# Experts of two latent tiles by a streamed table and dense gates, the other tiles by gathers

## The chip, the cores and the metric

One core of a Trainium2 chip. The metric is the device time of the whole program in microseconds. The program is one launch; all operands are fp32.

## The reference

One step of a layer for two groups of tokens: one tile of 128 context tokens and four tiles of 128 latent tokens, D_MODEL 1024. Two mixers (a gated recurrence and a windowed attention) and an output projection come first; the part that the change touches is the last one, a mixture over 16384 single-row experts, of which each token uses 16 in each of 8 heads:

```python
def per_block(xb):                      # 128 tokens
    q = (xb @ w_q).reshape(n, P_HEADS, 2, P_QDIM // 2)
    s = jnp.einsum('nhpd,hpkd->nhpk', q, sub_keys)
    s1, i1 = lax.top_k(s[:, :, 0], P_TOPK)
    s2, i2 = lax.top_k(s[:, :, 1], P_TOPK)
    cand_s = s1[..., :, None] + s2[..., None, :]
    cand_i = i1[..., :, None] * P_NKEYS + i2[..., None, :]
    top_s, pos = lax.top_k(cand_s, P_TOPK)         # both reshaped to (n, 8, 256)
    idx = jnp.take_along_axis(cand_i, pos, axis=-1)
    g = jax.nn.softmax(top_s, axis=-1)
    act = gelu(einsum('nhkd,nd->nhk', w_u[idx], xb))
    return einsum('nhk,nhkd->nd', g * act, w_v[idx])
```

Then x = x + gate2 * that, and a final RMSNorm. An expert's number is i1 * 128 + i2. w_u and w_v have 16384 rows of 4 KB, 64 MiB each.

## The kernel before

Five instruction streams (PE, ACT, DVE, POOL and SP) are written by hand and meet in semaphores. The order of PE's work is one list of names (`NAMES`, from `plan_groups`): each name is one accumulation group in PSUM, such as `("y", q, t)` (a 256-column quarter of the output projection of tile t), `x2T` and `h2` (transposes around the second norm), `qp` and `ss` (queries and scores of one half of a head). Groups take PSUM banks 0 to 3 in turn, and whoever evicts a group frees its bank.

Weights come as slabs of 1 MiB through a ring of three slots in SBUF (`SLABS`, issued by SP; a slot is loaded again when PE has finished the last group that reads it).

The experts are done by slots. A slot is one (head, k) of one tile: 128 indices, one for each token. POOL issues an indirect DMA that brings the rows `[u | v]` of the 128 experts, 128 x 8 KB; DVE makes the dot product of u with h2 (`dot`, line 1412, into `apre`); ACT makes the gelu (line 957) and the weight (line 963, `wexp`); then v times the weight is added up. For tile 0 and every other slot of the first half of tile 1, DVE does this (`v_row`, line 1440); elsewhere ACT makes a diagonal matrix of the weights (line 973) and PE multiplies it with the v rows into PSUM (line 600, and 587 in the first half of tile 1). One tile has 128 slots, the five tiles 640.

A head's indices and gates come from `route_parts`, 12 parts on DVE (max, max_index, match_replace over the scores, sums of candidates, and two 128 x 864 products with a compare to pick the expert's number); they are laid between the slots of the heads before.

Slots that run beside other work are placed by `STAGES`: a stage is a stretch of the list of names with a count of slots and a share for each kind of name, and every engine does slot n before the name where the plan puts it (`Beside`). ACT and DVE have slots and groups in one program order. Tile 0's 128 slots run beside the latent tiles' input projection, mixers and mix. 64 slots of tile 1 run beside `post(1)` (tile 1) and `post(2)` (tiles 2, 3, 4). Then come loops with the last 448 slots alone, with eight gather buffers, three of them in the slab ring. Gathers beside other work have four buffers (`NGA`) for tile 0 and six for tile 1. `tile_end(t)` adds the result to x and does the final norm, five operations of 128 x 1024.

Of the kernel before, what the change touches and what calls it, by code (L numbers as in the profile page):

```python
# [54 lines left out]
NGA, NGC, NGB = 4, 6, 8  # L55
HSTATIC = 4
NPE = HSTATIC * TOPK // 2
HSLOTS = 2 * TOPK
# [11 lines left out]
BATCHES = [(0,), (1,), (2, 3, 4)]  # L70
MIXES = [(0,), (1, 2, 3, 4)]
NSLOT = TSLOT + HSTATIC * TOPK
# [6 lines left out]
FIRST_ODD = 9  # L79
# [9 lines left out]
POOL_LEAD, PE_LAG = 3, 2  # L89
# [3 lines left out]
for _b in range(len(BATCHES)):  # L93
    if _b < len(MIXES):
        for _q in range(4):
            SLABS += [("gate_a", _b, _q), ("gate_b", _b, _q), ("wo", _b, _q)]
    SLABS += [("wout", _b, _q) for _q in range(4)] + [("wpq", _b, _q) for _q in range(8)]
    if _b == 0:
        SLABS += [("winTL", w, m) for w in WIN_T for m in range(2)] + [("winL", w, a) for w, a in WIN]

# [19 lines left out]
def turn_order(tiles):  # L120

    order = []
    for i in range(len(tiles) + 1):
        order.extend([("x2T", tiles[i])] if i < len(tiles) else [])
        order.extend([("h2", tiles[i - 1])] if i else [])
    return order


def plan_groups():
# [35 lines left out]
    def post(b):  # L165
        tiles = BATCHES[b]
        names.extend(("y", q, t) for q in range(4) for t in tiles)
        names.extend(turn_order(tiles))
# [34 lines left out]
    for b in (1, 2):  # L203
        marks.append(len(names))
        post(b)
    marks.append(len(names))
    marks.insert(-2, names.index(("ss", 1, FIRST_ODD)))
    place, used, fulls, n, six = {}, [0] * 6, [0] * 6, 0, 0
    for name in names:
        kind = name[0]  # L210
        wide = kind in ("xT", "kT", "dS", "qkT", "x2T", "h2") or (kind in ("sc", "pT") and name[1] >= HB)
# [27 lines left out]
    for (_, count, share), lo, hi in zip(STAGES, marks, marks[1:]):  # L239
        reach = np.cumsum([share[names[i][0]] for i in range(lo, hi)])  # L240
# [14 lines left out]
def build(nc, x_prompt, x_sample, cols, rows, normf_rows, brow, consts, masks, sel, cond_rows, ada_slabs, col_slabs, in_slabs, o_slabs,  # L255
          out_slabs, pq_slabs, uv, state, ckT, cv, y_prompt, y_sample, new_state, new_k, new_v):
    with ExitStack() as ctx:
# [17 lines left out]
        R1 = sb("R1", [P, 4 * D])  # L275
# [5 lines left out]
        RG = sb("RG", [P, 3 * 2 * D])  # L281
        BP = sb("BP", [P, NT * 256 + 6 * 512])
        AB = sb("AB", [P, 12288])
        HG = sb("HG", [P, 5632])
# [4 lines left out]
        CT = sb("CT", [P, P + 640 + NCAND])  # L289
# [6 lines left out]
        hst = sb("hst", [P, 16])  # L296
        ast = sb("ast", [P, 168])
        ZB = sb("ZB", [P, P], BF16)
# [6 lines left out]
        ident, mbias, iota = CT[:, 0:P], CT[:, P:P + 640], CT[:, P + 640:P + 640 + NCAND]  # L305
# [60 lines left out]
        XN2 = [view(HG, 0, D), view(HG, D, D)]  # L366
        SQ2 = [view(HG, 4096, D), view(HG, D, D), view(HG, D, D)]
        QP = [view(HG, 5120, 2, P), view(HG, 4096, 2, P), view(HG, 4096, 2, NB[2])]
        X1 = [XP] + [AB[:, 6144 + i * D:6144 + (i + 1) * D] for i in range(4)]
        H2 = [PB[:, 0:D]] + [AB[:, at:at + D] for at in (0, 3072, 4096, 5120)]  # L370
        SC = [R1[:, 0:2048], HG[:, 2048:4096], R1[:, 0:2048], AB[:, 10240:12288], AB[:, 1024:3072]]

# [151 lines left out]
        def _(sp):  # L524
# [1392 lines left out]
```

## Time and profile before

| | us |
|---|---|
| median of 3 runs | 2536.47 |
| lowest, highest | 2534.52, 2538.31 |
| span of the profiled execution | 2543.3 |

No time of its own is recorded for the profiled execution beside its span, from the first to the last instruction; the span lies 6.8 us above the median. Busy time in it: PE 2005.6 us (79%), DVE 1749.4 (69%), ACT 945.2 (37%), POOL 941.2 (37%). DMA moved 805.53 MB. In the slices of the page each digit is a fortieth of the span, 63.6 us. A matmul of fp32 appears as two records.

### The profile page before, as it was taken

To read this page: it belongs to the slowest core of one execution; us is meant where nothing else is said; L and a number is where in the kernel's file an instruction comes from. 1 tells how busy PE (TensorE), PEld (TensorE's weight loads), DVE (VectorE), ACT (ScalarE), POOL (GpSimd) and SP (SyncE) were. 2 spreads that over 40 slices of the span, in tenths; PEclk is the share of its full clock that TensorE was granted. 3 is DMA by queue.
4 is the path that set the end of the run, shared out by engine and by line. 5 is a ranking of instruction groups with operands and counts; after the bars stand their busy time and mean duration, and the time that the engine had idled before them with its cause. 6 is when DMAs were issued, how large, how long until landed. Compare 5 with 4: busy or idle time off the path is not lost. (4 is left out here: it accounts for less than half of the span.)

```text
span 2543.3 us, 27323 instructions
## 1 busy us (share of the span) xinstructions
PE 2005.6 (79%) x6925; PEld 1104.9 (43%) x6925; DVE 1749.4 (69%) x3969; ACT 945.2 (37%) x2456; POOL 941.2 (37%) x774
## 2 busy tenths in 40 slices
PE   6978898946677798668698776877768787687876
PEld 2577846745566543267455222322223222232222
DVE  2732278886776678767787777777777777777764
ACT  1402145223343434312333444444444444344443
POOL 0020012232222222303233554656545665456654
PEclk9998999977888899879899998999999999999999
DMA  8744678851111389859798999999999999999997
GB/s 317 289 152 154 231 291 322 332 192 67 67 67 60 150 332 337 337 203 401 272 372 317 422 421 393 420 422 422 421 404 415 422 422 421 407 401 421 422 422 330
DMA packets 113299, 805.53 MB, mean 317 GB/s; under 512 B 12596, under 2 KB 14006, under 8 KB 17046
## 3 DMA queue, kind: packets, MB, share of 16 engines
q0 software_dynamic: 93760, 680.96, 66.5%
q1 hardware_dynamic: 17704, 118.17, 12.6%
q10 hardware_dynamic: 1712, 4.98, 0.5%
q8 instruction: 50, 0.82, 0.1%
q14 instruction: 73, 0.60, 0.1%
HBM read 800.79 MB, written 3.28 MB: 316 GB/s over the span
## 5 line engine op out<-in xcount | busy, mean ns | idle before, releaser
L1213 POOL DMA_INDIRECT RG<-in_uv,idxs x264 | 356.5, 1351 | 562.0 <-DVE pl L1440 322.1
L957 ACT ACTIVATE agel<-apre 128x1 f32<-128x1 f32 x640 | 129.3, 202 | 984.6 <-DVE apre L1412 981.2
L600 PE MATMUL pl<-RG,BP 128*128 128x512 f32 x576 | 294.9, 638 | 106.8 <-ACT BP L973 102.3
L600 PE MATMUL pl<-RING,BP 128*128 128x512 f32 x576 | 281.7, 621 | 62.1 <-ACT BP L973 59.6
L1412 DVE CUSTOM_DVE_ANT_0 R<-RG,AB 128x1024 f32<-128x1024 f32 x201 | 246.8, 1230 | 100.8 <-DMA RG<-in_uv,idxs 79.8
L1213 POOL DMA_INDIRECT RING<-in_uv,idxs x168 | 248.9, 1482 | 158.7 <-PE pl L600 69.4
L1412 DVE CUSTOM_DVE_ANT_0 R<-RING,AB 128x1024 f32<-128x1024 f32 x168 | 205.9, 1226 | 95.6 <-DMA RING<-in_uv,idxs 77.2
L625 PE MATMUL pa<-HL,RING 128*128 128x512 f32 (+2 forms) x800 | 243.7, 461 | 4.2 <-DVEq L457 2.6
L600 PEld LDWEIGHTS pl<-RG,BP 128*128 128x128 f32 x576 | 100.1, 192 | 294.5 <-ACT BP L973 214.0
L973 ACT ACTIVATE BP<-CT,wexp 128x128 f32<-128x128 f32 x480 | 192.7, 401 | 51.1 <-PE pl L600 12.9
L600 PEld LDWEIGHTS pl<-RING,BP 128*128 128x128 f32 x576 | 104.3, 194 | 234.2 <-ACT BP L973 139.7
L963 ACT ACTIVATE wexp<-agel,gws 128x1 f32<-128x1 f32 x640 | 188.7, 295 | 22.4 <-ACT agel L957 0.3
L625 PEld LDWEIGHTS pa<-HL,RING 128*128 128x128 f32 x800 | 134.5, 195 | 106.0 <-issue 74.3
L1213 POOL DMA_INDIRECT EB<-in_uv,idxs x88 | 118.3, 1345 | 147.0 <-DVE pl L1440 96.8
L1440 DVE SCALAR_TENSOR_TENSOR pl<-RG,wexp,pl 128x1024 f32<-128x1024 f32 x118 | 151.6, 1285 | 9.6 <-ACT wexp L963 9.5
L1412 DVE CUSTOM_DVE_ANT_0 R<-RG,BP 128x1024 f32<-128x1024 f32 x96 | 117.7, 1226 | 43.4 <-DMA RG<-in_uv,idxs 27.6
L1412 DVE CUSTOM_DVE_ANT_0 R<-EB,AB 128x1024 f32<-128x1024 f32 x67 | 82.4, 1229 | 60.1 <-DMA EB<-in_uv,idxs 58.0
L625 PE MATMUL pa<-RING,AB 128*128 128x256 f32 (+2 forms) x432 | 103.9, 390 | 14.8 <-DVEq L457 10.3
L600 PE MATMUL pl<-HL,BP 128*128 128x512 f32 x192 | 94.9, 617 | 24.9 <-ACT BP L973 22.2
L957 ACT ACT_TABLE_LOAD x86 | 110.3, 1283 | 9.9 <-ACT RING L1096 2.8
L600 PE MATMUL pl<-EB,BP 128*128 128x512 f32 x192 | 98.8, 639 | 11.1 <-ACT BP L973 11.1
L625 PEld LDWEIGHTS pa<-RING,AB 128*128 128x128 f32 (+1 forms) x432 | 82.9, 201 | 34.1 <-issue 17.3
(288 smaller groups left out, 3261.0 us busy)
## 6 DMA issues: line engine op xcount, KB each, us to landing
RING<-in_in_slabs SPq DMA_DIRECT2D x42, 1024.0 KB, 6.0
RING<-in_pq_slabs SPq DMA_DIRECT2D x24, 1152.0 KB, 5.5
RING<-in_ada_slabs SPq DMA_DIRECT2D x16, 1024.0 KB, 5.0
RING<-in_out_slabs SPq DMA_DIRECT2D x12, 1024.0 KB, 9.1
RG<-in_col_slabs POOLq DMA_DIRECT2D x8, 1024.0 KB, 6.9
RING<-in_o_slabs SPq DMA_DIRECT2D x8, 1024.0 KB
RG<-in_uv,idxs POOLq DMA_INDIRECT x297
RING<-in_uv,idxs POOLq DMA_INDIRECT x168
```

The lines of the kernel that those rows point to most:

```text
L600: last = nc.tensor.matmul(acc[:, c * 512:(c + 1) * 512], DG[:, k % 2, :], bufs[k % len(bufs)][:, D + c * 512:D + (c + 1) * 512], start=Fal ...
L625: return nc.tensor.matmul(out, l, r, start=s, stop=e)
L957: A(agel[:, par, k:k + 1], apre[:, par, k:k + 1], ACT.Gelu).then_inc(gel_done, 1)
L963: A(wexp[:, par, k:k + 1], agel[:, par, k:k + 1], ACT.Copy, scale=gws[:, par, k:k + 1]).then_inc(w_done, 1)
L973: A(DG[:, i % 2, :], ident, ACT.Copy, scale=wexp[:, par, k:k + 1]).then_inc(dg_done, 1)
L1213: nc.gpsimd.indirect_dma_start(out=bufs[b], out_offset=None, in_=uv, in_offset=bass.IndirectOffsetOnAxis(ap=idxs[:, par, k:k + 1], axis=0) ...
L1412: V.tensor_tensor_reduce(out=SCR[k % 2], in0=buf[:, 0:D], in1=hc, scale=1.0, scalar=0.0, op0=ALU.mult, op1=ALU.add, accum_out=apre[:, par, ...
L1440: V.scalar_tensor_tensor(PL[:, :], (GC[i % NGC] if t else GA[n % NGA])[:, D:2 * D], wexp[:, n // TOPK % 2, n % TOPK:n % TOPK + 1], PL[:, : ...
```

## The change

- Tiles 2 and 4 (`DENSE`) don't gather any more. All 16384 experts are computed for their 256 tokens, in 128 chunks; chunk c holds the 128 experts whose second key is c, one for each partition (first key). `u_slabs` and `v_slabs` are the two tables laid out by chunk, two chunks a slab, and go through the slab ring after the other weights.
- `experts_u(c)`: 8 matmuls of 256 columns and a gelu on ACT into `AR`, a ring of 50 chunks in SBUF. `experts_v(c)`: 4 matmuls of 512 columns that add `AR` times v into PSUM banks 4 to 7.
- The gates: routing in DVE (`dense_route`, with the expert's number kept as a value); `slots_of` splits the number in two keys; PE turns the three tables so that tokens lie on columns (`T`); for each token, POOL makes a one-hot of the first keys times the weight (`OH1`, for the odd groups of tile 4 DVE does it, `drawn`), DVE one of the second keys (`OH2`), and one matmul of 128 columns (`G`, four tokens a group) gives the 128 x 128 gates of the token. ACT puts them in a staging buffer, 16 tokens with all chunks, and stores it to DRAM (`gates`), 1 MiB at a time, with 16 tokens inside and the chunks outside. SP loads them block by block (16 chunks of one tile, 1 MiB), and DVE multiplies them into `AR` (`weigh`, 2048 elements a partition).
- Tiles 1 and 3 gather all their 128 slots, each with dot and v row on DVE, in four buffers; PE and the diagonals have no part in slots any more. 256 slots follow those of tile 0: 26 beside `post(2)`, 24 beside the stage `early`, 206 beside the stage `dense`.
- `BATCHES` are (0), (1, 2), (3, 4). The scores are copied by ACT. x of the latent tiles is stored to DRAM and loaded again near the end. `tile_end(0)` stands before `post(1)`; tile 1's in the middle of the slots; tiles 3, 2 and 4 at the end.

The core of the diff:

```diff
+NGA, NGD = 4, 4
+DENSE, GATHERED = (2, 4), (0, 1, 3)
+NCH, NEARLY, NRING = NKEYS, 34, 50
+NFREE = 24
+GBLK, GTOK = 16, 16
-BATCHES = [(0,), (1,), (2, 3, 4)]
+BATCHES = [(0,), (1, 2), (3, 4)]
...
-          ("post1", 0, {"y": 3.5, "x2T": 2.0, "h2": 2.0, "qp": 2.0, "ss": 1.0}),
-          ("queries1", 4, {"qp": 2.0, "ss": 0.1}),
-          ("post2", 60, {"y": 3.4, "x2T": 2.5, "h2": 2.5, "qp": 5.2, "ss": 1.2}))
+          ("post1", 0, {}),
+          ("post2", 26, {"y": 3.4, "x2T": 2.5, "h2": 2.5, "qp": 5.2, "ss": 1.2}),
+          ("early", 24, {"U": 3.4, "T": 1.0, "G": 1.6}),
+          ("dense", 206, {"V": 1.0, "U": 1.0}))
+NAHEAD = 3
+SLABS += [("dU", p) for p in range(NRING // 2)]
+for _p in range(NCH // 2):
+    SLABS += [("dV", _p)] + ([("dU", _p + NRING // 2)] if _p + NRING // 2 < NCH // 2 else [])
...
+    at = {("dU", NEARLY // 2 + 2): [(0, 0), (0, 1)], ("dU", NRING // 2 - 2): [(1, 0)], ("dU", NRING // 2 - 1): [(1, 1)]}
+    for b in range(2, NBLK):
+        for i, back in enumerate((7, 6)):
+            at[("dV", GBLK // 2 * b - back)] = [(b, i)]
...
+DENSE_AT = {("U", 2 * (d - NAHEAD)) if d < PH else ("G", 0, 4 * (d - PH)): d for d in range(NAHEAD, 2 * PH)}
...
+def early_order():
+    order, c = [("U", n) for n in range(10)], 10
+    for i in range(ND):
+        order.append(("T", i))
+        for h in range(PH):
+            order.extend(("G", i, 4 * h + x) for x in range(4))
+            upto = 10 + 14 * (h + 1) // PH if i == 0 else NFREE + (NEARLY - NFREE) * (h + 1) // PH
+            order.extend(("U", n) for n in range(c, upto))
+            c = upto
+    return order + [("U", n) for n in range(NEARLY, NRING)]
...
+            def gate_slab(b, i):                                   # SP
+                n = b * ND + i
+                if n == 0:
+                    wait_full(sp, ("G", ND - 1, P // 4 - 1))
+                    for s in stage_out:
+                        sp.wait_ge(s, 16 * (ND * P // GTOK // 2))
+                if n >= 2:
+                    sp.wait_ge(p_done, n - 1)
+                sp.dma_start(GS[n % 2], gates[b, i]).then_inc(gate_in[n % 2], 16)
...
+            def experts_v(c):                                      # PE
+                w = slab("dV", c // 2)[:, c % 2 * D:(c % 2 + 1) * D]
+                if c % GBLK == 0:
+                    pe.wait_ge(p_done, ND * (c // GBLK + 1))
+                for i in range(ND):
+                    for x in range(2):
+                        last = nc.tensor.matmul(VACC[i][:, x * 512:(x + 1) * 512], AR[:, c % NRING, i * P:(i + 1) * P],
+                                                w[:, x * 512:(x + 1) * 512], start=c == 0, stop=c == NCH - 1,
+                                                skip_group_check=True)
+                last.then_inc(vd_done, 1)
...
+            def gates_out(i, g):                                   # ACT
+                to = STG[s].rearrange("p b (c t) -> p (b c) t", c=GBLK)[:, :, g % 4 * 4:g % 4 * 4 + 4]
+                step(A(to, ps.rearrange("p (t n) -> p n t", t=4), ACT.Copy), *freed(("G", i, g)))
+                if g % 4 == 3:
+                    at = g // 4 * GTOK * GBLK
+                    act.dma_start(gates[:, i, :, at:at + GTOK * GBLK].rearrange("b p n -> p b n"),
+                                  STG[s]).then_inc(stage_out[s], 16)
...
+                for x in range(ONEHOT):                            # POOL, slot_hots
+                    at = q * ONEHOT + x
+                    step.post(nc.gpsimd.tensor_scalar(OH1[n % 2][:, x, :], iota_p, SLT[i][:, 0, at:at + 1],
+                                                      SLT[i][:, 2, at:at + 1], ALU.is_equal, ALU.mult))
...
+            def weigh(b, i):                                       # DVE
+                dve.wait_ge(act_ready, GBLK * (b + 1))
+                dve.wait_ge(gate_in[n % 2], 16 * (n // 2 + 1))
+                gate = GS[n % 2].rearrange("p (a c t) -> p c a t", c=GBLK, t=GTOK)
...
+                    step(V.tensor_tensor(to, to, gate[:, lo:lo + m], ALU.mult))
...
+            for name in early_order():                             # DVE
+                if name[0] == "T" or name in DENSE_AT:
+                    beside.before(name)
+                    beside.clear()
+                if name in DENSE_AT:
+                    dense_route(DENSE_AT[name])
+                if name[0] == "T":
+                    weights_of(PH * (name[1] + 1) - 1)
+                    slots_of(name[1])
+                if name[0] == "G" and name[2] % 2 == 0:
+                    beside.before(name)
+                    gate_hots(name[1], name[2] // 2)
+            beside.before(("U", NRING - 4))
+            weigh(0, 0)
+            weigh(0, 1)
...
+            for b in range(2, NBLK):
+                beside.before(("V", GBLK * b - 8))
+                weigh(b, 0)
+                weigh(b, 1)
+            beside.rest()
+            for e in range(2, NT):
+                tile_end(e)
```

## Rows read from the trace of the kernel before

**Rows 1.** The page: busy time, slices of DMA and GB/s, the last chain.

```profile
span 2543.3 us, 27323 instructions
...
DMA  8744678851111389859798999999999999999997
GB/s 317 289 152 154 231 291 322 332 192 67 67 67 60 150 332 337 337 203 401 272 372 317 422 421 393 420 422 422 421 404 415 422 422 421 407 401 421 422 422 330
...
DMA 15%; issue 9%; DVE 5%; POOL 5%; PE 3%; ACT 2%; DVEq 0%; POOLq 0%; ACTq 0%
```

**Rows 2.** Windows: length, busy by engine, PE clock, DMA share, GB/s.

```profile
1386.00:2530.00 1144.00, 892.10 (x1847) 324.82 (x1846) 818.90 (x1983) 495.55 (x1467) 654.28 (x448) 0.97 1.00 414
950.00:1050.00 100.00, 88.37 (x199) 37.42 (x198) 79.67 (x128) 38.05 (x77) 27.18 (x26) 0.97 0.91 341
1097.00:1386.00 289.00, 253.22 (x1073) 177.15 (x1072) 221.16 (x518) 84.72 (x235) 68.91 (x65) 0.93 0.83 320
```

**Rows 3.** Timeline of PE at post(1): start, length, records.

```profile
1094.58 16.55 PE L625 MATMUL pa<-RING,AB 128*128 128x256 f32 x64
1115.12 1.97 PE L628 MATMUL pa<-CT,HG 128*128 128x128 f32 x8 [3.99 <-DVEq L457]
...
1121.05 4.94 PE L625 MATMUL pa<-HL,RING 128*128 128x128 f32 x32
```

**Rows 4.** Timeline of PE, runs of 256, 512 and 128 columns.

```profile
499.50 7.07 PE L625 MATMUL po<-RING,HL 128*128 128x256 f32 x32
506.41 7.07 PE L625 MATMUL pa<-RING,HL 128*128 128x256 f32 x32
...
1295.11 1.88 PE L587 MATMUL po<-EB,BP 128*128 128x512 f32 x4
1296.83 0.83 PE L625 MATMUL pa<-RING,HG 128*128 128x128 f32 x6
```

**Rows 5.** Timeline of DVE, a slot with dot and v row.

```profile
363.08 1.23 DVE L1412 CUSTOM_DVE_ANT_0 R<-RG,BP 128x1024 f32<-128x1024 f32 x1 [0.25 <-DVE idxs L1379]
...
365.43 1.22 DVE L1412 CUSTOM_DVE_ANT_0 R<-RG,BP 128x1024 f32<-128x1024 f32 x1
```

**Rows 6.** Timeline of DVE, route(0), 34 operations; first, compare and last.

```profile
323.14 0.29 DVE L1350 COPY BP<-R 128x256 f32<-128x256 f32 x1
323.58 0.29 DVE L1332 MAX8 BP<-BP 128x8 f32<-128x128 f32 x1
...
332.30 1.06 DVE L1372 TENSOR_TENSOR BP<-CT,BP 128x864 f32<-128x864 f32 x1
...
336.09 0.23 DVE L1389 TENSOR_SCALAR gws<-BP 128x16 f32<-128x16 f32 x1
```

**Rows 7.** DMA issues of the page: the norm row, median us to landing.

```profile
R<-in_normf_rows ACTq DMA_DIRECT2D x5, 512.0 KB, 7.9
```

**Rows 8.** Groups of POOL: busy us, mean ns.

```profile
L1263 POOL TENSOR_SCALAR HG<-AB 128x512 f32<-128x512 f32 x4 | 2.5, 619 | 11.7 <-PE pa L628 11.7
...
L1255 POOL TENSOR_TENSOR CO<-HG 128x4 f32<-128x4 f32 x5 | 1.0, 200 | 0.4
```

**Rows 9.** Timeline of DVE and SP, the last `tile_end` and store.

```profile
2534.30 1.23 DVE L1698 TENSOR_TENSOR R<-pl,G 128x1024 f32<-128x1024 f32 x1 [3.59 <-PE pl L894]
...
2538.87 1.28 DVE L1706 SCALAR_TENSOR_TENSOR AB<-AB,st,R 128x1024 f32<-128x1024 f32 x1
2540.24 0.33 SPq L570 DMA_DIRECT2D out<-AB  x1
```

**Rows 10.** Windows with slabs and gathers mixed, columns as in rows 2.

```profile
1144.00:1208.00 64.00, 56.16 (x269) 45.33 (x268) 49.06 (x124) 15.41 (x46) 20.59 (x20) 0.95 0.99 401
1290.00:1340.00 50.00, 50.00 (x172) 29.39 (x171) 43.12 (x100) 16.08 (x47) 18.26 (x16) 1.00 0.98 382
```

**Rows 11.** Timeline, one gather buffer's turn: v row, issue, dot.

```profile
1057.21 1.28 DVE L1440 SCALAR_TENSOR_TENSOR pl<-EB,wexp,pl 128x1024 f32<-128x1024 f32 x1
1058.49 1.22 DVE L1412 CUSTOM_DVE_ANT_0 R<-RG,BP 128x1024 f32<-128x1024 f32 x1
...
1064.85 1.23 DVE L1412 CUSTOM_DVE_ANT_0 R<-EB,BP 128x1024 f32<-128x1024 f32 x1 [0.39 <-DMA EB<-in_uv,idxs]
...
1059.30 1.22 POOL L1213 DMA_INDIRECT EB<-in_uv,idxs  x1 [2.90 <-DVE pl L1440]
```

**Rows 12.** The dots' line from 930 to 1090 us, and SP's issues.

```profile
L1412 DVE DVE_READ_ACCUMULATOR2_ANT apre<- x42: 76/83/85, 932.9 to 1088.4; 128x1 f32 x42
...
1026.73 74.40 SPq L558 DMA_DIRECT2D RING<-in_out_slabs  x4
```

More of the change, by code:

```diff
@@ L475, in open, with clear @@
             def open(self, t):
-                self.first, self.end = t * TSLOT, min((t + 1) * TSLOT, NSLOT)
+                self.first, self.end = (0, TSLOT) if t == 0 else (TSLOT, NSLOT)
+            def clear(self):
+                while self.next < self.end and self.next % TOPK in (3, 4):
+                    self.slot(self.next)
+                    self.next += 1
             def rest(self):
@@ L513, in half_update, with drawn, pool_hots, block_of @@
             yield mul(tots[:, set_of(u), d, :] if l == LEVELS - 1 else HT[d][l % 2][:, 0:n], T2[:, :, 0], T2[:, :, 1])
+        def drawn(i, q):
+            return i == ND - 1 and q % 2 == 1
+        def pool_hots(i, q):
+            return sum(not drawn(a, b) for a in range(ND) for b in range(P // ONEHOT) if (a, b) < (i, q)) + 1
+        def block_of(i, g):
+            n = i * (P // GTOK) + g * 4 // GTOK
+            return n % 2, n // 2
         slab_turn, counts = {}, [0] * NSLAB
@@ L889, in post, with experts_u @@
                     finish(("ss", b, m), last)
[L891 to L897 removed]
+            def experts_u(c):
+                w = slab("dU", c // 2)[:, c % 2 * D:(c % 2 + 1) * D]
+                ps = start(("U", c))
+                for k in range(KD):
+                    last = mm(ps[:, 0:DTOK].rearrange("p (t n) -> p t n", t=ND), w[:, k * P:(k + 1) * P],
+                              hTl[:, k, :].rearrange("p (t a n) -> p t a n", t=ND, a=2)[:, :, 1, :], k == 0, k == KD - 1)
+                finish(("U", c), last)
@@ L1143, in post, with scores_out @@
                         step(A(H2[t], ps, ACT.Copy), *freed(("h2", t)), h2_ready)
+                def scores_out(m):
+                    ps = group(("ss", b, m))
+                    for i, t in enumerate(tiles):
+                        step.post(A(SC[t][:, m * NKEYS:(m + 1) * NKEYS], ps[:, i * NKEYS:(i + 1) * NKEYS], ACT.Copy))
+                    step.settle(*freed(("ss", b, m)), sc_ready)
                 if b == 1:
-                    tile_root(0)
+                    act.wait_ge(v_done, TSLOT + V0)
+                if b == 2:
+                    act.wait_ge(x1_early, 32)
                 for m in range(2 * PH):
@@ L1802, in _ @@
             beside.rest()
+            tile_end(0)
+            post(1)
+            dve.wait_ge(kv_out, 32)
+            dve.wait_ge(sc_ready, 2 * PH + 2)
+            route(PH, 0, 12)
+            dve.wait_ge(sc_ready, 2 * PH + 4)
+            route(PH + 1, 0, EARLY)
+            step(V.memset(ACC, 0.0))
+            for d in range(NAHEAD):
+                dense_route(d)
             beside.open(1)
-            post(1)
             post(2)
-            beside.rest()
-            dve.wait_ge(h2_ready, NT)
@@ L1838, in shape_constants @@
+            beside.before(("U", NRING - 4))
+            weigh(0, 0)
+            weigh(0, 1)
+            beside.before(("V", 4))
+            weigh(1, 0)
+            weigh(1, 1)
+            for b in range(2, NBLK):
+                beside.before(("V", GBLK * b - 8))
+                weigh(b, 0)
+                weigh(b, 1)
+            beside.rest()
+            for e in range(2, NT):
+                tile_end(e)
 def shape_constants():
```

720 lines of the change are left out of this document (371 added, 349 removed).

## The prediction

> **What bounds the kernel now.** I read the page first. Its slices [rows 1] show three regimes: up to the twentieth slice DMA is mostly unsaturated, then two slices of change, and from the 23rd on DMA is at 9 tenths with 401 to 422 GB/s, while PE, DVE, ACT and POOL all have gaps. The chain that ended last says the same: its largest share is DMA, in gathers. Next the windows by stage [rows 2]: from 1386 us to 2530 us the DMA share is 1.00 at 414 GB/s, DVE is busy 72% and PE 78%. So the tail, 45% of the span, is a pure gather stream: 448 of the 640 slots (a slot is one expert row of u and v for each of 128 tokens, 128 x 8 KB = 1 MiB) at 1 MiB / 422 GB/s = 2.49 us each. Before it, from 1097 to 1386 us, the work after the mixers (output projection, second norm, queries) runs at 320 GB/s beside the first 64 slots of tile 1. Nothing before 1094 us depends on the change except ACT instead of DVE copying the scores of tile 0 and a few moved buffers: I cost that at nothing (the copies wait for PE either way; the bound is a microsecond or two either side).
>
> **What the change trades.** From 1094.6 us, where PE starts `y` of tile 1 [rows 3], before moves 512 MiB of gathers and 26 MiB of weight slabs. After moves 256 MiB of gathers (tiles 1 and 3), 26 of weights, 64 of u and 64 of v as slabs, 16 of gates out, 16 of gates in and some 6 of small things: 448 MiB = 470 MB. At 422 GB/s that is 1113 us against 1337. But half of the v rows move from PE to DVE, and tiles 2 and 4 bring new work on PE, so I go stage by stage, since the plan ties slots to PE's groups (ACT does both in one order, so neither may run far ahead).
>
> Unit costs. U chunk: 8 matmuls of 256 columns; 32 records (16 matmuls, each recorded twice) take 6.91 us to the next start [rows 4], so a chunk takes 3.45 us. V chunk: 4 matmuls of 512 columns; two take 1.72 us [rows 4], so 3.45 us. A 128-column matmul: 0.22 us [rows 4]. A gathered slot on DVE is now always dot and v row: 363.08 to 365.43 us, 2.35 us [rows 5], plus some 0.15 of waits. A head's routing run without a break takes from 323.14 to 336.3 us [rows 6]; the change drops the first copy (0.44 us): 12.8 us for a gathered head; a dense one drops the index cast too and adds nothing else: 12.5 us. So a gathered slot costs 2.5 + 12.8/16 = 3.3 us of DVE.
>
> **Stage A, post(1) with tiles 1 and 2, no slots.** PE: 8 groups `y` 27.7 us; the turn through the norm 9.9 us for one tile (1111.1 to 1121.05 [rows 3]), 12 for two; 16 x (3.45 + 0.44) = 62 us queries and scores. 1094.6 + 102 = 1197 us. `tile_end(0)` now stands ahead of `y` on DVE and waits for the norm row (7.9 us to landing [rows 7], formerly hidden): DVE is free at about 1106 us; PE fills its four banks until 1108 us, so this costs nothing; at worst 5 us. DVE then does route(8), half of route(9), a memset and three dense routes, from 1143 us when the first two scores are there: 12.8 + 6.5 + 0.9 + 37.5 gives 1201 us. Even with PE.
>
> **Stage B, post(2) with tiles 3 and 4, 26 slots.** PE 102 us again, from 1201; `y` is slowed by five slots between its reads, and the 19 slots beside the queries cost DVE 19 x 3.3 = 63 us, as much as PE's 62. End about 1310 us.
>
> **Stage C, 50 U chunks and the gates, 24 slots.** PE: 50 x 3.45 + 256 gate matmuls x 0.22 = 229 us. DVE: 13 dense routes x 12.5 = 162; 19 slots before the last gate group x 3.3 = 63; 32 one-hots of 128 x 1024: a form like the 864 wide compare, 1.06 us [rows 6], scaled 1.25 + 0.1 = 1.35, 43 us; 8 x 2 more for the drawn ones, 22; the slots of two tiles made ready and turned, with the round trips through PE and ACT, 11 by estimate (ten 128 wide operations of some 0.3 us a tile [rows 6] and 2.5 us of trip). Sum 301 us. So C is DVE's: 1310 + 301 = 1611 us for the last gate group; PE waits at `T`. POOL builds 24 x 8 one-hots; an operation of 512 wide takes 0.62 us [rows 8], 128 wide between 0.2, the smallest POOL row [rows 8], and 0.62: at most 5 us per eight tokens against DVE's 9 per eight: hidden (if not, 24 x a few us). Then PE has 16 U chunks left, 55 us, and ahead of chunk 38 SP's queue holds the first two gate loads, which wait for the last gate store: some 10 us of bubble. V starts at about 1678 us.
>
> **Stage D, 128 V and 78 U chunks, 206 slots.** Three bounds. PE: 206 x 3.45 = 711 us. DVE: 206 x 3.3 = 680, `weigh` 16 x 2.4 (2048 elements, twice the 1.22 us of a 1024 wide one [rows 9]) = 38, `tile_end(1)` 8: 726. DMA: 206 gathers, 39 + 64 slabs, 12 gates, 2 for x: 323 MiB, less 6 already in flight or landed: 317 MiB = 332 MB. At the 422 GB/s of the tail's slices [rows 1] 788 us. So DMA bounds D whatever it does, and the question is the rate. Rows for mixed traffic [rows 10]: 401 GB/s at a share of 0.99 (1144 to 1208 us, gathers in six buffers with slabs), 382 at 0.98 (1290 to 1340), 341 at 0.91 in the mix stage [rows 2], where gathers have four buffers as they will here: 829, 870 and 975 us. D keeps three slab slots and four gathers wanting all the time, and both other engines are at 0.86 to 0.88 of its length, so I take the row where DMA was really full, 401: 829 us.
>
> Do four buffers let it be full? The buffer's v row is done one slot after its dot, so only three gathers run ahead. From the v row's end at 1058.49 to the gather's issue at 1059.30 is 0.8 us, from there to its dot at 1064.85 us 5.55 us [rows 11], with DMA lightly loaded; dot and v row 2.4 more: 8.8 us for three slots, 2.9 us a slot. D wants 829/206 = 4.0 us a slot, 12 us for three, so each gather may stand 3 us in the queue behind a slab. That is enough for a steady stream, not for the 5 us of two `weigh`.
> The Trainium skill ("DMA: Bandwidth & Descriptors", the section on issuing engines) says that transfers started by scalar, sync and gpsimd run on the same 16 engines and interleave. By that rule slabs and gathers share one rate, as I have them; a second stream on top would leave D at 726 us, and no run here shows such a thing.
>
> **The end.** After the last gather: dot, weight, v row 3 us; three `tile_end` in a row instead of one, 2534.30 to 2540.15 = 5.9 us each [rows 9], 18; store 3: 24 us.
>
> **Sum.** 1678 + 829 + 24 = 2531 us against the span of 2543.3. The profiled execution lies 6.8 us above the median of 2536.5 shown, so I take the same off: about 2525 us, 0.5% faster. Most of the 224 us that the smaller traffic would give are lost because A to C move only some 130 MiB in 583 us.
>
> **Rivals.**
> 1. D at a mixed rate of 390 to 422 GB/s, as forecast: D 788 to 851 us, 2484 to 2547 us. For it: the 64 us at 401. Chance 0.5 (0.4 of it faster, 0.1 within 0.2%).
> 2. Slower: the four gather buffers and the lock step through ACT leave DMA idle part of the time. For it: the mix stage, also with four buffers, where 42 dots took 160 us, 3.8 us each, at 341 GB/s [rows 12]. Against: slabs were rare there, four in 74 us [rows 12], so nothing else filled the gaps. At 341 to 385 GB/s D takes 862 to 975 us: 2558 to 2671 us. It decides from 393 GB/s downward (2542 us). Chance 0.3. The skill's page on DMA (Bandwidth) gives about 358 GB/s as what HBM leaves one core; by that D would take 927 us and end near 2623; the tail's 422 GB/s disagrees, and I give it no chance of its own.
> 3. Slower: C is longer. If POOL's one-hots cost more than 0.62 us each, or DVE waits for ACT's exponentials, gelus and slots in turn, 30 to 60 us more: 2555 to 2585. Against: hots are double buffered and routes stand between. Chance 0.1.
> 4. Clearly faster: A to C end 30 us or more earlier, because PE runs its U chunks under the routes, and D runs at 422: 2440 to 2470 us. Chance 0.1.
>
> **Numbers.** The likeliest is 2525, its own range 2484 to 2547. 0.2% (5 us) is about what a measurement of this kernel can tell from no change. Faster 0.4 + 0.1 = 0.5, same 0.1, slower 0.3 + 0.1 = 0.4. For 8 in 10 I go from 2470 to 2605 (365 GB/s in D).
>
> **What would show it.** `V` starting near 1678 us; in C, DVE nearly full and PE waiting for it; in D, DMA share at 0.95 or more with 390 to 405 GB/s, DVE and PE both near 0.85, and dots that wait for gathers. Wrong it is if D's share of DMA is well under 0.95 (rival 2: buffers, or who waits for whom), if PE waits in C for POOL, if slabs and gathers together pass 405 GB/s, or if `weigh` over its 16-element runs takes far more than 2.4 us, 16 times on the path of V.

## The result, and the profile after

The changed kernel takes 2715.1 us (median of 4 runs, 2711.5 to 2722.9) against 2535.5 us: a ratio of 1.0708, 95% interval 1.0689 to 1.0727. It is 7.1% slower, where I had forecast 2525 us and a range up to 2605. Two of the runs below, with five buffers and with the shifted slots, had one execution each in a slower state (4211.9 and 3080.0 us), which their times here leave out.

The page of the changed kernel: slices of 1/40 of the span, the chain that ended last by engine, and two of its groups (count | busy us, mean ns | idle before, and its releaser):

```profile
span 2710.9 us, 28055 instructions
...
DMA  7836598722113998444932445689999899999996
GB/s 310 294 115 220 204 351 331 277 92 70 63 47 141 352 344 311 140 187 171 384 142 93 155 148 187 234 333 385 397 359 393 338 401 359 391 377 381 383 351 234
...
DMA 28%; DVE 25%; PE 21%; issue 16%; POOL 7%; ACT 2%; DVEq 1%; POOLq 0%; ACTq 0%; SPq 0%
...
L1371 POOL DMA_INDIRECT R<-in_uv,idxs x288 | 323.1, 1122 | 1138.5 <-DVE AB L1620 729.5
...
L710 PE MATMUL pa<-XS,EB 128*128 128x128 f32 x512 | 92.0, 360 | 130.5 <-POOLq L530 73.8
```

The slices answer [rows 1]: the flat 420 GB/s of the gather stream from the 23rd slice on has gone. In its place stand ten slices (17th to 26th) in which DMA is at 2 to 6 tenths but for one, and then a stretch at 8 to 9 tenths that moves 338 to 401 GB/s, where the kernel before moved 393 to 422 (its 25th slice has 393, which I had read over). POOL stood idle 729.5 us for v rows before it could issue gathers into `R`, and the gate matmuls (`pa<-XS,EB`) waited 73.8 us for POOL's queue. The windows of the changed kernel (us, then busy time of PE, PEld, DVE, ACT, POOL, then granted clock, DMA share, GB/s), gate stage and V stage, to be held against [rows 2]:

```profile
1445.00:1729.00 284.00, 170.52 (x865) 155.06 (x866) 186.26 (x410) 78.27 (x149) 216.98 (x193) 0.79 0.47 157
1791.00:2659.00 868.00, 749.19 (x2275) 447.46 (x2274) 612.43 (x1044) 157.80 (x522) 214.16 (x199) 0.94 0.95 374
```

**Where the 180 us are.** My sum was 2531 us against this span of 2710.9. For the milestones I split it where the trace can be read. `T` of tile 2 was due at 1388 us (my 1310 for the end of `post(2)`, five dense routes, three slots and half of the 11 us for turning the slots) and comes at 1427 (+39). From there to the end of the last gate group remain 223 us of my sum; it takes 302, to 1729 (+79). The U chunks between it and the first V take 62 us instead of 67 (-5). From the first V to the end of the last slot I had 829 us; it is 1791 to 2690, 899 (+70). The end is 21 us instead of 24 (-3). These are +180. Milestones of single traces are not exact to a microsecond: in the three later runs that change only what the V stage loads, gathers or weighs, the first V starts between 1799.9 and 1803.5 us, here at 1791.5.

Each large term has its cause in a few rows. First, VectorE in route(8), the last operation of part 10 and the first of part 11:

```profile
1147.40 0.17 DVE L1510 CAST idxs<-BP 128x16 int32<-128x16 f32 x1
1188.51 0.16 DVE L1514 RECIPROCAL BP<-BP 128x1 f32<-128x1 f32 x1 [40.93 <-ACT BP L1063]
```

VectorE stands idle for 40.93 us until ScalarE has made the exponential of head 8. ScalarE's program now does the whole of `post(1)`, all sixteen evictions of queries and scores, before `expos(PH)`. Then TensorE at the seam of post(1) and post(2), and at `T`:

```profile
1185.96 13.98 PE L710 MATMUL pa<-RING,AB 128*128 128x256 f32 x64
1234.92 16.54 PE L710 MATMUL pa<-RING,AB 128*128 128x256 f32 x64 [34.98 <-DVEq L530]
...
1427.09 0.90 PE L713 MATMUL pa<-CT,BP 128*128 128x128 f32 x3 [21.55 <-DVEq L1550]
1445.36 4.82 PE L710 MATMUL pa<-XS,EB 128*128 128x128 f32 x29 [17.37 <-issue]
```

It has filled four banks with `y` of `post(2)` and waits 35 us for VectorE, which is still routing: that is the first term. Second, the operations of POOL's one-hots (count: min/median/max ns, first and last start):

```profile
L1384 POOL TENSOR_SCALAR EB<-CT,BP x128: 780/790/2545, 1431.5 to 1595.5; 128x128 f32<-128x128 f32 x128
L1384 POOL TENSOR_SCALAR EB<-CT,RW x64: 785/1402/2543, 1608.6 to 1722.6; 128x128 f32<-128x128 f32 x64
```

and VectorE's waits from 1326 to 1785 us (us in total, times, longest):

```profile
DVE AB L1620 <- ACT wexp L1081: 54.6, 7, 15.6
DVE XS L1567 <- PE pa L710: 42.3, 14, 6.9
```

A weighted one-hot of 128 x 128 costs 0.79 to 1.40 us in the median, not at most 0.62: eight take 7.9 us by the mean in tile 2's half and 11 in tile 4's (10.9 for those at 1623 us). TensorE waits for them, and VectorE for TensorE (42.3 us) to free the one-hots' buffers. Third, one turn of a gather buffer in the V stage, on VectorE:

```profile
1964.70 1.28 DVE L1620 SCALAR_TENSOR_TENSOR AB<-R,wexp,AB 128x1024 f32<-128x1024 f32 x1
...
1975.70 1.23 DVE L1594 CUSTOM_DVE_ANT_0 R<-R,BP 128x1024 f32<-128x1024 f32 x1 [0.83 <-DMA R<-in_uv,idxs]
...
1981.10 1.28 DVE L1620 SCALAR_TENSOR_TENSOR AB<-R,wexp,AB 128x1024 f32<-128x1024 f32 x1
```

and on POOL:

```profile
1966.79 0.94 POOL L1371 DMA_INDIRECT R<-in_uv,idxs  x1 [2.74 <-DVE AB L1620]
```

The v row ends at 1965.98, the gather into its buffer is issued 0.8 us later, the dot on it starts 8.9 us after the issue (5.55 in [rows 11]), and the v row that frees the buffer again ends at 1982.38: four slots in 16.4 us, 4.1 us each.

### The profile page after: what moved, and what is told of

Its sections match the earlier page's. It is cut to its first block, busy times and chain, and to the rows that moved or that the text cites. A ratio compares the mean times of both kernels' runs of the same rounds, so it can differ in the third digit from the quotient of the medians.

```text
span 2710.9 us, 28055 instructions
## 1 busy us (share of the span) xinstructions
PE 2071.8 (76%) x8515; PEld 1462.2 (54%) x8515; DVE 1788.0 (66%) x3622; ACT 702.1 (26%) x1719; POOL 714.6 (26%) x713
## 4 chain that ended last, share of the span: by engine, by line
DMA 28%; DVE 25%; PE 21%; issue 16%; POOL 7%; ACT 2%; DVEq 1%; POOLq 0%; ACTq 0%; SPq 0%
DMA R<-in_uv,idxs 23%; PE pa L710 18%; POOL EB L1384 6%; DVE AB L1620 5%; DMA AB<-in_uv,idxs 4%; DVE pl L1620 4%; PE po L710 1%; PE pa L713 1%; DVE AB L1585 1%; DVE AB L1749 1%; DVE AB L1757 1%; DMA RING<-in_ada_slabs 1%; DVE BP L1499 1%; DVE BP L1496 1%; DVE apre L1594 1%
## 5 line engine op out<-in xcount | busy, mean ns | idle before, releaser
L710 PE MATMUL pa<-HL,RING 128*128 128x256 f32 (+1 forms) x2848 | 735.3, 417 | 103.6 <-ACTq L530 100.5
L710 PEld LDWEIGHTS pa<-HL,RING 128*128 128x128 f32 x2848 | 559.9, 200 | 279.1 <-issue 206.5
L1371 POOL DMA_INDIRECT R<-in_uv,idxs x288 | 323.1, 1122 | 1138.5 <-DVE AB L1620 729.5
L1594 DVE CUSTOM_DVE_ANT_0 R<-R,BP 128x1024 f32<-128x1024 f32 x192 | 235.5, 1227 | 139.6 <-DMA R<-in_uv,idxs 98.8
L1620 DVE SCALAR_TENSOR_TENSOR AB<-R,wexp,AB 128x1024 f32<-128x1024 f32 x192 | 246.1, 1282 | 56.9 <-ACT wexp L1081 56.8
L994 PE MATMUL po<-RING,AB 128*128 128x512 f32 x512 | 244.5, 600 | 36.0 <-DVEq L1587 36.0
L994 PE MATMUL pl<-RING,AB 128*128 128x512 f32 x512 | 241.4, 594 | 0.0
L710 PE MATMUL pa<-XS,EB 128*128 128x128 f32 x512 | 92.0, 360 | 130.5 <-POOLq L530 73.8
L710 PE MATMUL pa<-RING,AB 128*128 128x256 f32 (+3 forms) x528 | 125.0, 386 | 81.2 <-DVEq L530 77.4
L1384 POOL TENSOR_SCALAR EB<-CT,BP 128x128 f32<-128x128 f32 x128 | 124.6, 983 | 18.2 <-PE pa L710 16.5
L1620 DVE SCALAR_TENSOR_TENSOR pl<-R,wexp,pl 128x1024 f32<-128x1024 f32 x96 | 123.3, 1285 | 4.8 <-ACT wexp L1081 4.6
```

What stands on the lines that cost most here:

```text
L710: return nc.tensor.matmul(out, l, r, start=s, stop=e)
L994: last = nc.tensor.matmul(VACC[i][:, x * 512:(x + 1) * 512], AR[:, c % NRING, i * P:(i + 1) * P], w[:, x * 512:(x + 1) * 512], start=c == ...
L1371: nc.gpsimd.indirect_dma_start(out=bufs[b], out_offset=None, in_=uv, in_offset=bass.IndirectOffsetOnAxis(ap=idxs[:, par, k:k + 1], axis=0) ...
L1384: step.post(nc.gpsimd.tensor_scalar(OH1[n % 2][:, x, :], iota_p, SLT[i][:, 0, at:at + 1], SLT[i][:, 2, at:at + 1], ALU.is_equal, ALU.mult))
L1594: V.tensor_tensor_reduce(out=SCR[k % 2], in0=bufs[b][:, 0:D], in1=hc, scale=1.0, scalar=0.0, op0=ALU.mult, op1=ALU.add, accum_out=apre[:, ...
L1620: V.scalar_tensor_tensor(acc, (GD[(n - TSLOT) % NGD] if s else GA[n % NGA])[:, D:2 * D], wexp[:, n // TOPK % 2, n % TOPK:n % TOPK + 1], ac ...
```

## The experiments

Theories: **A**, ScalarE's order costs the first term and GpSimd's one-hots the second. **B**, these waits only cover work of VectorE that would bound those stages anyway. For the V stage: **C**, slabs and gathers mixed move no more than 374 GB/s; **D**, the turn of four gather buffers paces it. All kernels start from the changed one; three of them combine edits. V stage below is from the start of the first V to the start of the last, from the trace: 864 us in the changed kernel (868 with the last matmuls, as in the window above). The runs were made at different times, and the kernel before, run beside them, took 2532.9 to 2537.6 us; so a difference of two times is good to some 5 us, and the ratio to the kernel before is the safer number.

**1. Early exponentials.**

```diff
                     if m:
                         scores_out(m - 1)
+                    if b == 1 and m == 6:
+                        expos(PH)
+                    if b == 1 and m in (11, 15):
+                        dense_expos((m - 11) // 4)
...
             post(1)
-            expos(PH)
-            for d in range(NAHEAD):
-                dense_expos(d)
+            dense_expos(NAHEAD - 1)
```

> Only ScalarE's program order is changed: the exponential of head 0 of tile 1 stands behind the seventh group of queries of post(1), and those of the first two dense heads behind the twelfth and the last, as the kernel before had its one. Theory A (the wait of 41 us on VectorE in part 11 of route(8) is ScalarE's order alone): the wait falls to under 6 us, y of post(2) starts some 35 us earlier (near 1200 us instead of 1235), and since nothing behind it is changed, V starts near 1756 instead of 1791 and the kernel takes 2675 to 2690 us. Rival B (the time is given back, because the next stages are paced by something with its own clock): VectorE's wait goes, V moves by less than 15 us, 2700 to 2715 us.

2686.6 us, ratio 1.0601 (1.0558 to 1.0643). The same wait of VectorE (1085 to 1300 us; in total, times, longest):

```profile
DVE BP L1516 <- ACT BP L1063: 5.1, 1, 5.1
```

and TensorE at the seam:

```profile
1187.32 28.08 PE L710 MATMUL pa<-RING,AB 128*128 128x256 f32 x128
1234.16 3.68 PE L713 MATMUL pa<-CT,AB 128*128 128x128 f32 x16 [18.77 <-DVEq L530]
```

All eight groups of `y` follow without a gap, `T` of tile 2 comes at 1392.5 instead of 1427.1, V at 1762.4 instead of 1791.3, and the kernel is 28.5 us faster. Theory A holds for the first term. This is one edit in the order of one engine that is busy 26% of the span.

**2. What GpSimd's one-hots cost.** One of eight drawn, and two ways to spread them:

```diff
-                for x in range(ONEHOT):
+                for x in range(1):
```

> GpSimd draws only one of the eight weighted one-hots of each group; the other seven keep old contents, so the gates are not the reference's, and all counts and waits stay. Theory A (GpSimd's one-hots pace the gate stage): the stage from the first to the last G falls from 284 us to 215 to 240, TensorE's waits for GpSimd (74 us) go to under 10, V starts at 1735 to 1750 us, and the kernel takes 2655 to 2675 us. Rival B (VectorE, with its routes, slots and waits for ScalarE's weights, paces it): the stage is 265 us or more, and the kernel at 2695 to 2715 us. VectorE's small operations beside it should fall from 0.25-0.32 us back to 0.18 if the two engines share something, and stay if not.

2654.8 us, ratio 1.0478 (1.0439 to 1.0516), 60 us faster. The gate stage's window, from the first gate group to the last:

```profile
1447.00:1668.00 221.00, 157.80 (x875) 143.18 (x876) 177.10 (x408) 79.29 (x150) 41.43 (x38) 0.83 0.58 195
```

TensorE's wait for POOL in it is down from 73.8 to 7.8 us. One small operation of VectorE there (busy, mean ns), without the one-hots and then, in the changed kernel, with them:

```profile
L1483 DVE CAST CT<-CT 128x32 f32<-128x32 uint32 x8 | 1.5, 183 | 0.3
```

```profile
L1483 DVE CAST CT<-CT 128x32 f32<-128x32 uint32 x8 | 2.4, 299 | 0.3
```

221 us instead of 284. My 223 count from `T` of tile 2, which comes 17 us before the first gate group: by that measure the stage falls from 302 to 236 us (1430.5 to 1666.5), 13 above the forecast. Theory A holds, and B falls as the account of the 79 us; for the 13 that are left it is not refuted, for VectorE still waits 42.2 us for ScalarE's weights of slots there, where my sum had 0.15 us a slot. The traced execution is the fastest of this run's five (2642.3 us).

```diff
-                    step.post(nc.gpsimd.tensor_scalar(OH1[n % 2][:, x, :], iota_p, SLT[i][:, 0, at:at + 1],
-                                                      SLT[i][:, 2, at:at + 1], ALU.is_equal, ALU.mult))
+                w = SLT[i][:, 2, q * ONEHOT:(q + 1) * ONEHOT].unsqueeze(2).to_broadcast([P, ONEHOT, P])
+                pool.wait_ge(oh1d_ready, n + 1)
+                step(nc.gpsimd.tensor_tensor(OH1[n % 2], OH1[n % 2], w, ALU.mult), oh1_ready)
...
-                if drawn(i, q):
-                    step(V.tensor_tensor(OH1[n % 2], keys, slot_row(0), ALU.is_equal))
-                    step(V.tensor_tensor(OH1[n % 2], OH1[n % 2], slot_row(2), ALU.mult), oh1d_ready)
+                step(V.tensor_tensor(OH1[n % 2], keys, slot_row(0), ALU.is_equal), oh1d_ready)
```

`drawn` returns False here.

> VectorE compares for all 32 groups of eight tokens (one 128 x 1024 compare more for 24 groups, and no multiply for 8 of them: 30 us more and 11 less), GpSimd multiplies the weights in with one 128 x 1024 operation, by its 1.27 us for 512 elements about 2.5 us, instead of eight of 0.78 to 2.5 us. Theory A (GpSimd paces the gate stage): 32 x 2.5 = 80 us of GpSimd instead of 213; the stage falls to 235 to 255 us and the kernel to 2675 to 2695. Rival B (VectorE paces it): its 19 us more are added, 2725 to 2735 us.

2710.9 us, ratio 1.0701 (1.0660 to 1.0742): neither theory's number, and not told from the changed kernel. POOL's groups (busy, mean ns, idle before):

```profile
L1384 POOL TENSOR_TENSOR EB<-EB,RW 128x1024 f32<-128x1024 f32 x16 | 37.5, 2343 | 32.3 <-DVEq L530 32.3
L1384 POOL TENSOR_TENSOR EB<-EB,BP 128x1024 f32<-128x1024 f32 x16 | 37.5, 2343 | 127.0 <-DVEq L530 127.0
```

POOL's work falls to 75 us, as expected, but now it waits 159 us for VectorE's compare, and TensorE waits 132 us for POOL: a chain of three engines in a row for each group. Here less work for the pacing engine was worth nothing, since it was made to wait in return.

```diff
         def drawn(i, q):
-            return i == ND - 1 and q % 2 == 1
+            return True
```

> VectorE draws all one-hots, GpSimd none: 24 x 2.6 = 62 us more on VectorE, 213 us fewer on GpSimd. Theory A (GpSimd paces it, and slows VectorE beside it): VectorE was idle for 80 of the stage's 284 us, so it takes most of it in, stage 270 to 290 us, kernel 2700 to 2720. Rival B (VectorE paces it): 50 to 60 us longer, 2765 to 2775 us.

2703.4 us, ratio 1.0671 (1.0627 to 1.0715), in theory A's range of 2700 to 2720 and far from B's 2765 to 2775, but again hardly told from the changed kernel. What counts is where: from `T` of tile 2 to `T` of tile 4 the time rises from 180 to 202 us (VectorE has eight dense routes there), from there to the start of the last gates it falls from 116 to 88 us. So:

```diff
-            return i == ND - 1 and q % 2 == 1
+            return i == ND - 1
```

together with the early exponentials of run 1.

> ScalarE's order as in the run with early exponentials (28.5 us there), and VectorE draws the one-hots of all 16 groups of tile 4, GpSimd those of tile 2. Theory A (in tile 4's half of the gate stage the cycle of 15 us a pair is GpSimd's, 10.9 us for eight plus a gather, while VectorE idles 42 us): the cycle falls to 11 us, 8 x 4 = 32 us less, kernel 2650 to 2665 us. Rival B (VectorE has no room): 0 to 10 us less than 2686.6.

2644.3 us, ratio 1.0425 (1.0401 to 1.0449), 42 us less than run 1 and 6 below the range of theory A. The second half is 88 us again, V starts at 1730.8 instead of run 1's 1762.4 (32 us). Of the other 10 us, 6 lie in the V stage (862 us, 868 in run 1), without a cause that I know; the rest is no more than the two traced executions differ from their medians.

**3. What paces the V stage.** Three buffers instead of four (and POOL two slots ahead instead of three):

```diff
-NGA, NGD = 4, 4
-        GD = GA[:3] + [view(ABH, NRING * DTOK + 3 * D, 2 * D)]
+NGA, NGD = 4, 3
+        GD = GA[:3]
```

> Three gather buffers for tiles 1 and 3 instead of four, and GpSimd's gathers placed two slots ahead instead of three; only the stage from the first V to the last (868 us after the change) is judged. Theory C (the stage is bounded by the transfers' rate: DMA was 94 to 96% full at 374 GB/s): it stays within 15 us, since a slot has 4.2 us there. Theory D (the turn of a gather buffer and the lock step of the engines bound it): two slots ahead instead of three over a turn of 8.8 us makes at least 4.4 us a slot, and the bubbles grow: 910 to 960 us, DMA share under 0.9.

2925.7 us (one run). V stage 1028 us instead of 864: theory D, and more of it than the 910 to 960 I had expected, which took the turn of 8.8 us from a lightly loaded stretch. Then `weigh` cut short:

```diff
+                    to, by = to[:, 0:1], gate[:, lo:lo + 1]
-                    step(V.tensor_tensor(to, to, gate[:, lo:lo + m], ALU.mult))
+                    step(V.tensor_tensor(to, to, by, ALU.mult))
```

> VectorE weighs one chunk of the 16 (each piece of weigh does 128 values instead of up to 2048), so that the experts' sums of tiles 2 and 4 are not the reference's; transfers, waits and counts stay. Theory C (transfers' rate): the V stage stays within 12 us of 868, kernel 2700 to 2715 us. Theory D (stalls: a gather can't be issued while VectorE weighs, and TensorE waits for ScalarE, which waits for VectorE's dot): 16 x 2.1 us of VectorE and the stalls of 18 us before the first V of blocks go, V stage 820 to 840, kernel 2665 to 2685.

2696.1 us, ratio 1.0635 (1.0609 to 1.0661). V stage 837 us, 27 less, at 387 GB/s: the stage is theory D's number, the kernel lies between the two, since V started 8 us later. Tile 3's gathers at half the row:

```diff
+                w, src = (D, uv.rearrange("n (a d) -> (n a) d", a=2)) if n >= 2 * TSLOT else (2 * D, uv)
-                    out=bufs[b], out_offset=None, in_=uv,
+                    out=bufs[b][:, 0:w], out_offset=None, in_=src,
```

> The gathers of tile 3 bring rows of 4 KB instead of 8, by the same indices over a table of half rows: wrong rows, and the v halves are stale; 128 x 0.5 MiB = 67 MB less, all within the V stage. Tile 3's stretch there is some 550 us, 4.3 us a slot. Theory C (transfers' rate): 67 MB at 374 GB/s are 179 us, of which the next bounds (3.45 us of TensorE a slot, 3.3 of VectorE) leave 90 to 110, V stage 755 to 780 us, DMA share under 0.85 in tile 3's stretch. Theory D (engines in lock step): V stage 820 or more.

2655.0 us (one run). V stage 806 us: 58 less of the 179 that 67 MB would be worth at 374 GB/s, with the DMA share at 0.83 from 2100 us on. Both numbers missed: a third of what the rate alone would give came, and yet the stage ran below theory D's 820 us. The trace shows why: the gathers of 4 KB rows land in 6.4 us (66 into `R`) and 5.2 us (22 into `AB`) in the median between 2160 and 2500 us, those of tile 1 with 8 KB rows in 10.1 and 9.9 us between 1830 and 2080. So this edit shortens the turn as well as the traffic and cannot tell C from D by itself.

The loads of v halved:

```diff
-                sp.dma_start(at[:, 0:SLOTW if kind == "wpq" else SLAB], src).then_inc(s, 16)
+                w = SLOTW if kind == "wpq" else SLAB // 2 if kind == "dV" else SLAB
+                sp.dma_start(at[:, 0:w], src[:, 0:w] if kind == "dV" else src).then_inc(s, 16)
```

> Only the first half of each v slab is loaded (512 KB instead of 1 MiB), the other chunk is stale, so the sums of tiles 2 and 4 are not the reference's; 33.5 MB less in the V stage. Theory C (transfers' rate): 33.5 MB at 374 GB/s, 90 us less, V stage 770 to 790 us. Theory D (turn of the gather buffers): a slab of half the size makes a gather stand shorter in the queue, but its own transfer stays; 30 to 60 us less, 810 to 840 us.

2673.4 us (one run). V stage 818 us, 47 less and not 90: theory D's range. The upward test decides:

```diff
-        GD = GA[:3] + [view(ABH, NRING * DTOK + 3 * D, 2 * D)]
+        GD = GA[:3] + [view(ABH, NRING * DTOK + 3 * D, 2 * D), R1[:, 0:2 * D]]
...
-                V.tensor_tensor_reduce(out=SCR[k % 2], in0=bufs[b][:, 0:D], in1=hc, scale=1.0, scalar=0.0,
+                V.tensor_tensor_reduce(out=bufs[b][:, 0:D] if bufs is GD else SCR[k % 2], in0=bufs[b][:, 0:D], in1=hc, scale=1.0, scalar=0.0,
```

GpSimd goes four slots ahead instead of three there, and `tile_end` takes its scratch row from `ACC`.

> The changed kernel with a fifth gather buffer for tiles 1 and 3 (the dots write their products over the u half they have read, so the two scratch rows are free for it) and GpSimd four slots ahead instead of three. Theory D (the turn of a buffer, some 12.7 us under load for three slots, is what paces the V stage at 4.2 us a slot): the turn now covers four slots, 3.2 us, the transfers' own rate takes over, 325 MB at 395 to 400 GB/s: V stage 815 to 830 us instead of 868, DMA share 0.98 or more; the gate stage gains under 10 us; kernel 2660 to 2680 us. Theory C (the rate of slabs and gathers together is 374 GB/s however many buffers there are): V stage 855 or more, kernel 2700 to 2715.

2642.0 us, ratio 1.0421 (1.0401 to 1.0440), 73 us faster, and better than the 2660 to 2680 of theory D: the V stage is 800 us, 64 less, and another 11 us of the span are saved behind the last V, where the last slots run. The V stage's windows with three, four (above) and five buffers:

```profile
1817.00:2848.00 1031.00, 797.51 (x2273) 480.18 (x2271) 606.40 (x1037) 156.59 (x517) 200.51 (x196) 0.88 0.84 313
```

```profile
1791.00:2595.00 804.00, 736.25 (x2277) 441.44 (x2275) 618.75 (x1053) 159.46 (x528) 216.87 (x201) 0.96 0.99 407
```

313, 374 and 407 GB/s. By the dots in these windows (193, 195 and 198; the other 15 to 10 of tile 3 come after the last V) a slot takes 5.3, 4.5 and 4.1 us in the mean, and from dot to dot 5.2, 4.2 and 3.8 in the median. Theory C falls: the same mixture moves 407 GB/s once there is something to issue. The landing times of the gathers (median us from issue, 1900 to 2500 us) with three and with four buffers:

```profile
R<-in_uv,idxs POOLq DMA_INDIRECT x114, 6.7
```

```profile
R<-in_uv,idxs POOLq DMA_INDIRECT x101, 9.3
...
AB<-in_uv,idxs POOLq DMA_INDIRECT x34, 8.1
```

With three, 0.8 + 6.7 + 2.4 = 9.9 us for two slots, 5.0 each by this estimate, against the median of 5.2. With four, 0.8 + 9.0 (the two rows weighted) + 2.4 = 12.2 for three, 4.1 each, against 4.2. The means lie higher by the stalls below. The landing time grew with what was in flight, from 6.7 to 9.0 us for one buffer more, and the share read 0.95 while the stage was still short of buffers.

**4. All of it together.** Runs 1, 2 and the fifth buffer in one, and then with 16 slots moved from the V stage to the two before it:

> Early exponentials, VectorE's one-hots for tile 4, and the fifth gather buffer. If the three causes add up: 2644 less what the fifth buffer gives alone, so 2590 to 2610 us by theory D and 2630 to 2645 by theory C. Still slower than the kernel before (2536) by either, for what is left is VectorE's own work from 1100 us to the first V.

2569.3 us, ratio 1.0129 (1.0106 to 1.0152): 146 us less than the changed kernel, where the three steps gave 28.5 + 42.3 + 73.1 = 144, and below the 2590 to 2610 that I had expected. `T` of tile 2 is at 1388.0 us, V from 1722.2 to 2519.8.

```diff
-          ("post2", 26, {"y": 3.4, "x2T": 2.5, "h2": 2.5, "qp": 5.2, "ss": 1.2}),
-          ("early", 24, {"U": 3.4, "T": 1.0, "G": 1.6}),
-          ("dense", 206, {"V": 1.0, "U": 1.0}))
+          ("post2", 34, {"y": 3.4, "x2T": 2.5, "h2": 2.5, "qp": 5.2, "ss": 1.2}),
+          ("early", 32, {"U": 3.4, "T": 1.0, "G": 1.6}),
+          ("dense", 190, {"V": 1.0, "U": 1.0}))
```

> As the run with all three, and 16 slots are taken from the V stage (190 instead of 206) and put 8 each beside the queries of tiles 3 and 4 and beside the gate stage. If the early stages are VectorE's alone, each slot moved costs 3.3 us there and saves 4.0 in the V stage: 5 to 12 us less than with all three. If the early stages are paced by waits between engines that have room: 40 to 60 us less. If the moved slots lie on a chain of waits (weights, one-hots): 0 to 20 us more.

2564.7 us, ratio 1.0103 (1.0083 to 1.0123), not told from the run before. V starts 51 us later (1772.9) and its stage is 45 us shorter: a moved slot cost 3.2 us ahead of V, as expected, and saved 2.8 in it, not 4.0. None of the versions beats the kernel before.

## Why the prediction was wrong

The sum had three terms too small: VectorE's wait for ScalarE's exponential in A (taken at nothing), GpSimd's one-hots in C (taken as hidden), and the turn of the gather buffers in D (taken from an idle stretch). Rivals 2 and 3 named all three, but each with the rest of the sum as forecast; they came together, and 2715 us lies beyond either's range.

**Stage A.** The step that failed is "DVE then does route(8), half of route(9), a memset and three dense routes, from 1143 us". It added VectorE's own operations and took the exponential between parts 7 and 11 for free, without reading where the changed ScalarE puts it. Run 1 puts it back, and the stage meets the sum (`T` of tile 2 at 1392.5 against 1388, and 1388.0 in the combination). It is worth 28.5 us of kernel time. Routing also started at 1135 us, not 1143.

**Stage C.** The step "128 wide between 0.2, the smallest POOL row, and 0.62: at most 5 us per eight tokens against DVE's 9 per eight: hidden" failed twice. The upper bound was no bound: a row of 512 elements with constants says little of a 128 wide one that reads two scalars for each partition, and that took 0.79 to 1.40 us. And the cover is not there in tile 4's half: its dense routes are done by then, and VectorE has some 8 us of work for sixteen tokens, while POOL's eight one-hots (10.9 us), a gather (1.0) and the waits between make a cycle of 15 us for them. The price is 60 us of kernel time (run 2). Without the one-hots the stage takes 236 us from `T` on, still 13 above my 223; the wait of VectorE for ScalarE's weights (42.2 us in that trace) is the likeliest rest, but no run takes it away. My rival 3 named exactly this cost; I gave it 30 to 60 us and a chance of 0.1, too little for a cost that no row showed.

**From the last gate group to V** the time was near (62 us against 67) by two errors that cancel: eighteen chunks follow, not sixteen, for two of the 34 early ones come behind the last gates, and the bubble of 10 us from the gate loads did not come. The unit cost was right: 18 chunks in 62.3 us, 3.46 each.

```profile
1729.32 62.33 PE L710 MATMUL pa<-HL,RING 128*128 128x256 f32 x288
```

**Stage D.** The volume was right (371 GB/s from 1791 to 2690 us are 334 MB against my 332), and so was `weigh` (2.29 us against 2.4). What failed is "12 us for three, so each gather may stand 3 us in the queue behind a slab. That is enough for a steady stream". The 5.55 us from issue to dot came from a stretch where DMA was lightly loaded [rows 11]; under the load that D itself makes it is 8.9 us, which uses up the allowance of 3 us and leaves none for any stall. And D has stalls: at `tile_end(1)` POOL has nothing to issue for 10.66 us, and at the two `weigh` behind it for another 7.91:

```profile
2134.04 0.96 POOL L1371 DMA_INDIRECT AB<-in_uv,idxs  x1 [0.30 <-issue]
2145.66 0.94 POOL L1371 DMA_INDIRECT R<-in_uv,idxs  x1 [10.66 <-DVE AB L1620]
2154.50 1.18 POOL L1371 DMA_INDIRECT R<-in_uv,idxs  x1 [7.91 <-DVE AB L1620]
```

and the window between the two gaps (columns as above):

```profile
2145.00:2150.00 5.00, 5.00 (x15) 3.56 (x15) 4.33 (x7) 0.00 (x0) 0.94 (x1) 0.71 0.54 174
```

DMA moves 174 GB/s in it. TensorE, idle for 7.45 us until 2142.48 us because ScalarE waits for the same dot, has a granted clock of 0.50 (1.2 GHz) from 2140 to 2145 us and 1.00 again from 2150. Leaving `weigh` out gives back 27 us of the stage, the fifth buffer 64. With five buffers the slots take 1791 to 2614 us (span 2635.4 less the 21 us of the end), 823 us against my 829: the rate was right, for one buffer more than the kernel had. So rival 2 was the true course of this stage, with 371 to 374 GB/s in its range of 341 to 385. The stage costs some 70 us by it.

**The comparison of rates.** I took 401 GB/s from the row with six buffers and set the mix stage with four (341 GB/s, [rows 2, 12]) aside because "slabs were rare there". The nearest row by what was short, the buffers, was that one; the stage came between the two.

**What remains.** With the three causes mended the kernel is still 1.3% slower than before. It has 44 us more ahead of V than my sum (1722 against 1678). `T` of tile 2 is on time there (1388.0), so all of them lie behind it: 272 us to the end of the last gate group against 223, less the 5 of the U chunks. In its trace VectorE waits 51 us for ScalarE's weights of slots between 1085 and 1725 us, and TensorE 31 us for GpSimd's one-hots of tile 2. Neither was tried alone.

The Trainium skill ("GPSIMD Engine Reference", section 1, Specifications) says that GpSimd shares its SBUF interfaces with VectorE, with contention for VectorE's instructions in a 2-port perf mode or with two SBUF inputs. The trace agrees as far as it goes: VectorE's small cast took 299 ns in the mean beside the one-hots and 183 without, its two-input 128 x 864 products 1.12 and 1.16 us against 1.06. No run here shows that the interface is the reason.

## What to carry to other kernels

Judge a prefetch depth by the landing time under the load of the new stage, not by one read from an idle stretch: add the turn (free to issue, issue to landing, use), divide by the slots ahead, and compare with the time a slot has; a DMA share of 0.95 did not say here that buffers sufficed. When a small operation is moved to an engine that hardly works, look at the operation's own form for its price, and at what the engine stands between; when a wait between two engines crosses a stage, read the program order of the one that is waited for. Price each suspected cost by leaving it out before choosing where to put it: moving all one-hots to VectorE gained 12 us and splitting them between the two engines 4, neither clear of noise; the move placed by the trace gained 42.

## What the runs showed of the hardware

- GpSimd's `tensor_scalar` with two scalars for each partition took 0.78 us at best, 2.5 us at worst and 0.79 or 1.40 in the median of the two tiles for 128 x 128 fp32, while 128 x 512 with constants takes 0.62 [rows 8]. Its 128 x 1024 multiply took 2.34 us.
- VectorE's operations of 16 to 32 elements took 0.23 to 0.32 us in the mean beside these, and 0.18 to 0.23 where seven of eight were left out. Single ones of 16 elements took up to 0.73 us.
- Slabs of 1 MiB and indirect gathers of 128 rows of 8 KB together moved 407 GB/s at a share of 0.99, against 414 at 1.00 for the gathers alone [rows 2]; with gathers of 4 KB rows it was 298 GB/s at a share of 0.83, in a stretch where TensorE was busy 469 of 512 us.
- A gather of 128 rows of 8 KB landed 6.7 us after its issue with two ahead, beside slabs, and 9.0 us with three; with rows of 4 KB 6.1 us with three.
